# Row halves and column groups of TensorE for the small matmuls: softmax rounds over both KV groups, a reordered mLSTM output, and the router in four column groups

## The reference

```
proj = rms_norm(x) @ w_in            # attention q, k, v; mLSTM q, k, v, output gate; gates
att  = softmax(q k^T / 8 + bias, with a sink per head) v
                                     # 8 heads of 64, 2 KV groups of 4 heads, window of 128
h_m  = mLSTM(q_m, k_m, v_m, i, f)    # 4 heads, dqk 64, dv 128: per chunk
                                     #   num = scale * (q C) + (q k^T * decay) v, and its norm column
x    = x + concat(att, rms_norm(h_m) * sigmoid(o)) @ w_out
t    = rms_norm(x)
g_logits = t @ w_router_group        # 4 columns
e_logits = t @ w_router_expert       # 16 columns
x    = x + top-1 group, then top-2 of its 4 experts, SwiGLU experts of width 512
```

## Time and profile before

| | |
|---|---|
| median of 3 runs | 1065.3 us (1063.83 to 1066.48) |
| the profiled execution, its own time | 1064.2 us |
| its span in the profile | 1062.4 us |
| PE busy | 948.8 us, 89% |
| DVE busy | 618.2 us, 58% |
| ACT busy | 527.4 us, 50% |
| first stage (tiles) | up to about 433 us |
| second stage (output projection, router) | about 439 to 558 us |
| routing tables and first gather | about 553 to 590 us |
| experts | about 590 us to the end |
| granted TensorE clock, mean | 0.947 |

### The profile page before, as it was taken

One profiled execution on the slowest core, in us unless ns is written; L12 is line 12 of the kernel. 1 busy time (PEld: TensorE's weight loads), 2 busy tenths in 40 slices (PEclk: granted clock), 3 DMA queues, 4 the chain that ended last, 5 costly groups with the idle time before them and its releaser, 6 DMA issues. The chain is left out here.

```text
span 1062.4 us, 16918 instructions
## 1 busy us (share of the span) xinstructions
PE 948.8 (89%) x5026; PEld 792.8 (75%) x5027; DVE 618.2 (58%) x1245; ACT 527.4 (50%) x945; POOL 246.2 (23%) x362
## 2 busy tenths in 40 slices
PE   4789999999999969699971799999999999999993
PEld 3678889898888857588861577877877777787772
DVE  3646555656665565343367466447639489754891
ACT  3364644627455373122114356545638488664871
POOL 3101001010110100000017133243234345513452
PEclk9999999999999986899985799999999999999998
DMA  8620010101000050533463788678669799966963
GB/s 259 216 54 20 22 40 0 39 0 39 20 20 20 2 190 9 172 126 134 142 220 102 288 285 255 166 231 289 177 202 339 220 319 395 374 174 202 321 245 60
DMA packets 58122, 169.68 MB, mean 160 GB/s; under 512 B 12744, under 2 KB 15088, under 8 KB 58096
## 3 DMA queue, kind: packets, MB, share of 16 engines
q1 hardware_dynamic: 50384, 143.13, 37.5%
q0 software_dynamic: 7712, 26.24, 10.5%
HBM read 142.96 MB, written 26.38 MB: 159 GB/s over the span
## 5 line engine op out<-in xcount | busy, mean ns | idle before, releaser
L886 PE MATMUL bank_j<-w_high,rows_high 128*128 128x512 f32 x640 | 256.6, 401 | 11.7 <-DVE w_low L1327 9.4
L888 PE MATMUL bank_j<-w_high,rows_low 128*128 128x512 f32 x640 | 251.4, 393 | 0.0
L887 PE MATMUL bank_j<-w_low,rows_high 128*128 128x512 f32 x640 | 251.3, 393 | 0.0
L886 PEld LDWEIGHTS bank_j<-w_high,rows_high 128*128 128x128 f32 x640 | 121.2, 189 | 40.9 <-issue 12.3
L525 POOL TENSOR_TENSOR tick<-mhalf 1x1 f32<-1x1 f32 x146 | 83.9, 577 | 279.1 <-ACT lg L823 136.8
L888 PEld LDWEIGHTS bank_j<-w_high,rows_low 128*128 128x128 f32 x640 | 121.2, 189 | 26.1
L887 PEld LDWEIGHTS bank_j<-w_low,rows_high 128*128 128x128 f32 x640 | 121.6, 190 | 23.7
L1632 DVE TENSOR_TENSOR w_low<-w_res,w_high 128x1024 fp32r<-128x1024 f32 x96 | 112.8, 1219 | 13.8 <-ACT w_high L633 13.8
L633 ACT ACTIVATE w_high<-w_res 128x1024 fp32r<-128x1024 f32 x96 | 96.2, 1059 | 8.4 <-PE bank_j L888 8.0
L880 PE MATMUL bank_t<-ident,hn 128*128 128x128 f32 x328 | 45.1, 283 | 33.8 <-DMA hn<-ffn_in,row_g 22.2
L880 PEld LDWEIGHTS bank_t<-ident,hn 128*128 128x128 f32 x328 | 40.0, 146 | 39.0 <-issue 34.8
(11 more groups left out here) (301 smaller groups left out, 1823.0 us busy)
## 6 DMA issues: line engine op xcount, KB each, us to landing
w_res<-in_w_gate_dram SPq DMA_DIRECT2D x48, 512.0 KB, 4.9
w_res<-in_w_up_dram SPq DMA_DIRECT2D x48, 512.0 KB, 5.4
bias<-in_w_down_dram SPq DMA_DIRECT2D x32, 512.0 KB, 5.6
slot_b<-in_w_gate_dram SPq DMA_DIRECT2D x16, 512.0 KB, 5.7
PT<-in_w_up_dram SPq DMA_DIRECT2D x16, 512.0 KB, 5.9
gmix<-in_w_down_dram SPq DMA_DIRECT2D x16, 512.0 KB, 5.5
h<-in_w_down_dram SPq DMA_DIRECT2D x16, 512.0 KB, 7.2
hn<-in_x_dram SPq DMA_DIRECT2D x8, 512.0 KB, 3.5
```

The lines of the kernel that those rows point to most:

```text
L886: pe.matmul(out_, ah, bh, start=start, stop=False)
L887: pe.matmul(out_, ah, bl, start=False, stop=False)
L888: return pe.matmul(out_, al, bh, start=False, stop=stop)
```

## The change

Three edits, and what they need.

1. A softmax round r now holds two heads of each KV group: heads 2r and 2r+1 of group 0 (into S0) and of group 1 (into S1), and the matmuls alternate between the two row halves. `round_head` and `round_heads` give the head numbers and the strided slices of the per-head columns; `values`, `exps` and `logits` follow. The number and the sizes of the instructions on VectorE and ScalarE stay the same.
2. The mLSTM output first does the four products with 128 rows, then the four with 64 rows, which alternate between the row halves and the banks.
3. The router is turned round: its weights, padded from 20 to 32 columns, are stationary in one of four column groups (chunk k in group k % 4), the rows stream past, and the four partial sums land in four partition groups of X0[:, 0:128]. ScalarE copies them out (`router_parts`), and one more float32 matmul with a 0/1 matrix `rsel` adds them up (`router_sum`) into X0[:, 256:276]. For the tiles of the loop the router now stands before the second half of the output projection, its sum behind it. The padding of `wr` and the matrix `rsel` are made by GpSimd at the very start: two memsets and four affine selects more, and SyncE waits for them before it loads the router weights.

```diff
+        def round_head(r, j):
+            return (j // RH) * G + r * RH + j % RH          # RH = G // KVH = 2
+        def round_heads(per_head, r):
+            return per_head[:, :].rearrange("p (g r j) -> p g r j", g=KVH, r=G // RH)[:, :, r, :]
...
+            sp.wait_ge(pool_wr, 1)
...
+            chain(pool.memset(rsel[:, :], 0.0))
+            for q in range(4):
+                chain(pool.affine_select(out=rsel[:, :], in_=rsel[:, :], compare_op=ALU.not_equal, fill=1.0,
+                                         base=-q * WRC, pattern=[[-1, NG + NE]], channel_multiplier=1))
+            pool.memset(wr[:, :, NG + NE:], 0.0).then_inc(pool_wr, 1)
...
-                def scores(g, done):
-                    for j in range(G):
-                        b = (S0, S1)[j // 2]
+                def scores(r, done):
+                    for jj in range(RH):
                         for w, slot in ((0, v), (1, u)):
-                            c = (j % 2) * 2 * P + w * P
-                            ins = pe.matmul(b[:, c:c + P], qT[64 * g:64 * g + 64, j, :],
-                                            kTw[64 * g:64 * g + 64, slot, :], start=True, stop=True)
+                            c = jj * 2 * P + w * P
+                            for g, bank in enumerate((S0, S1)):
+                                ins = pe.matmul(bank[:, c:c + P], qT[64 * g:64 * g + 64, r * RH + jj, :],
+                                                kTw[64 * g:64 * g + 64, slot, :], start=True, stop=True)
...
                     for h in range(MH):
+                        c = h // 2
+                        pe.matmul((S0, S1)[h % 2][:, c * VE:(c + 1) * VE], sd[:, h, :], vm[:, h, :], start=(c == 0),
+                                  stop=False, skip_group_check=True)
+                    for h in range(MH):
                         r, c = 64 * (h % 2), h // 2
-                        o = (S0, S1)[h % 2][:, c * VE:(c + 1) * VE]
-                        pe.matmul(o, sd[:, h, :], vm[:, h, :], start=True, stop=False)
-                        ins = pe.matmul(o, qg[r:r + 64, c, :], Cst[r:r + 64, c, :], start=False, stop=True)
+                        ins = pe.matmul((S0, S1)[h % 2][:, c * VE:(c + 1) * VE], qg[r:r + 64, c, :], Cst[r:r + 64, c, :],
+                                        start=False, stop=True, skip_group_check=True)
...
                 for k in range(KC):
-                    ins = pe.matmul(X0[:, 0:NG + NE], h2T[:, k, :], wr[:, k, :], start=(k == 0), stop=(k == KC - 1))
-                ins.then_inc(pe_r, 1)
+                    q = k % 4
+                    ins = pe.matmul(X0[q * WRC:(q + 1) * WRC, 0:P], wr[:, k, :], h2T[:, k, :], start=(k < 4),
+                                    stop=(k >= KC - 4))
+                ins.then_inc(pe_rp, 1)
+
+            def router_sum(t):
+                pe.wait_ge(act_rp, t + 1)
+                pe.matmul(X0[:, 2 * P:2 * P + NG + NE], rpart[:, :], rsel[:, :], start=True,
+                          stop=True).then_inc(pe_r, 1)
...
                     mix_T(t + 1)
+                if not first and not last:
+                    router(t - 1)
                 if not first:
                     project_out(t, u, 1)
                 if last:
                     positions(TILES - 2, 1)
+                    router(t - 1)
                 if not first:
-                    router(t - 1)
+                    router_sum(t - 1)
...
+            def router_parts(t):                            # ScalarE, behind mix_high of body2
+                act.wait_ge(pe_rp, t + 1)
+                cp(rpart[:, :], X0[:, 0:P]).then_inc(act_rp, 1)
```

More of the change, by code:

```diff
@@ L116, in hymba_layer_program @@
         slot_b = sb("slot_b", [P, G * P + KVW + 64 + 2 * P + 2 * KVW])
-        wr = sb("wr", [P, KC, NG + NE])
+        WRC = P // 4
+        wr = sb("wr", [P, KC, WRC])
+        rpart = sb("rpart", [P, P])
+        rsel = sb("rsel", [P, NG + NE])
         ident = sb("ident", [P, P])
@@ L789, in body2 @@
                     mix_high(t + 1, 1 - u)
+                if not first:
+                    router_parts(t - 1)
                 act.wait_ge(dve_h, t + 1)
@@ L967, in probs_T, with values @@
                     ins.then_inc(done, 1)
-                def values(g, done):
+                def values(r, done):
                     for j in range(G):
-                        h = g * G + j
+                        h, g = round_head(r, j), j // RH
                         for w, slot in ((0, v), (1, u)):
@@ L1335, in out_low, with logits @@
                                          ALU.subtract).then_inc(lo0, 1)
-            def logits(t, g, s_done, l_done, nm_done):
-                hs = slice(g * G, g * G + G)
+            def logits(t, r, s_done, l_done, nm_done):
+                amx_r, anm_r, aes_r, sink_r = (round_heads(a, r) for a in (amx, anm, aes, sink))
                 dve.wait_ge(s_done, t + 1)
@@ L1348, in logits @@
                 dve.wait_ge(l_done, t + 1)
-                chain(dve.tensor_reduce(amx[:, hs], lg[:, :, :], AX, ALU.max))
-                chain(dve.tensor_tensor(amx[:, hs], amx[:, hs], sink[:, hs], ALU.max))
-                chain(dve.tensor_scalar(anm[:, hs], amx[:, hs], -1.0, None, ALU.mult))
-                dve.tensor_tensor(aes[:, hs], sink[:, hs], anm[:, hs], ALU.add).then_inc(nm_done, 1)
+                chain(dve.tensor_reduce(amx_r, lg[:, :, :].rearrange("p (g j) k -> p g j k", g=KVH), AX, ALU.max))
+                chain(dve.tensor_tensor(amx_r, amx_r, sink_r, ALU.max))
+                chain(dve.tensor_scalar(anm_r, amx_r, -1.0, None, ALU.mult))
+                dve.tensor_tensor(aes_r, sink_r, anm_r, ALU.add).then_inc(nm_done, 1)
             def body(t, u, main, nxt, ahead):
```

16 lines of the change are left out of this document (10 added, 6 removed).

## The result

The changed kernel takes 1034.6 us (median of 4 runs, 1031.3 to 1036.3), the kernel before beside it 1065.9 (4 runs, 1063.8 to 1067.9): ratio 0.9703, 95% interval 0.9672 to 0.9734. The prediction was 1033.0, with 1026 to 1042 as its range. The profiled execution took 1034.3 us, with a span of 1032.5.

What follows compares the result with a forecast made beforehand. TensorE, nearly always busy, was taken to bound the kernel. Savings of 22.3 + 3.3 + 5.0 + 1.7 = 32.3 us bring the profiled 1064.2 to 1031.9, forecast as a median of 1033.0 us, range 1026 to 1042.

Steps and rivals of the forecast that it cites:

- Score rounds: First-stage score rounds on TensorE: 1.98 to 1.09 us each, 0.2 us of waiting left, 1.58 us saved a tile.
- The bound of no overlap: Lower bound for the score rounds: saving 0 if the two row halves did not overlap.
- mLSTM output: First-stage mLSTM output group on TensorE: 3.29 to 1.67 us, saving 1.6 us, with VectorE still ready in time.
- Seven tiles: First-stage sum over seven tiles: 3.18 us saved in each, 22.3 us in all.
- Clock: First-stage tiles: one of three half-clock stretches fewer, 1.7 us saved; bounds 5.1 saved or several us lost.
- Last tile: Last first-stage tile: second score round saves 1.67 us, output 1.6, together 3.3; the DMA wait behind moves along.
- Second stage up to the tables: Second stage: five routers of 1.70 us become six of 0.68 and five sums, saving 3.3 us.
- The bound in which four column groups don't overlap: Second-stage router bound: all passes run singly, 2.2 us, a loss of 0.5 a tile.
- Tables: Routing tables: VectorE's wait of 1.39 us goes, plus some 0.3 of GpSimd's late wait of 0.66.
- Start: Program start: added GpSimd operations delay about 1.4 us, absorbed by TensorE's 1.49 us weight wait; cost 0, bounds 0 and 1.4.
- Other engines' chains: Rival, first stage: round 0's probabilities arrive too late, 0.7 us in seven tiles, 4.9 us back, 1038 us; chance 0.10.
- the rival: Clock falls oftener, in eight tiles and six router stretches: 11 falls more at 1.7 us, 1053 us; chance 0.08.

Runs made afterwards that it cites:

- e1: Kernel before with only the score rounds changed (both KV groups in alternating row halves): 1044.6 us, ratio 0.9825.
- e6: Changed kernel with each score round's matmuls not in turns, all of group 0 first, then group 1: 1039.4 us, ratio 0.9776 to the kernel before.
- e9: Kernel before with the new score rounds and the new mLSTM output order, without the router change: 1033.7 us, ratio 0.9733.
- e2: Kernel before with only the mLSTM output reordered (four products with 128 rows, then four with 64): 1060.0 us, ratio 0.9958.
- e10: The changed kernel measured again without any edit: 1028.9 us, ratio 0.9683 to the kernel before.
- e7: Changed kernel with all eight router matmuls in one column group and the sum over its 32 rows: 1044.5 us, ratio 0.9793 to the kernel before.
- e12: Changed kernel with ScalarE's copy of the router's partial sums moved behind the square, last body only: 1030.1 us, ratio 0.9671 to the kernel before.
- e4: Changed kernel with the six GpSimd operations moved from the start to behind the first tile's inverse root: 1028.7 us, ratio 0.9682 to the kernel before.
- e11: Changed kernel with the six GpSimd operations behind the first inverse root, measured again: 1028.4 us, ratio 0.968 to the kernel before.
- e5: Kernel before with only the six GpSimd operations at the start and the wait of the router's weight loads added: 1067.5 us, ratio 1.0007.
- e3: Kernel before with only the router changed, including its padding and `rsel`: 1063.5 us against 1066.3, ratio 0.9977.
- e8: Changed kernel with the router back behind the output projection's second half, its sum right behind it: 1032.9 us, ratio 0.9687 to the kernel before.

## Why the prediction was right, and where its steps were not

- **Score rounds: right.** 1.09 us and a wait of 0.18 for 1.09 and 0.2. e1 gives 1.64 us a tile, the step said 1.58. The bound of no overlap is excluded by e1, and e6 shows that the turns bring most of it. Line 1041 was the right row to go by. The Trainium skill, "TensorE: Matmul & The Clock Gate", Part 3, gives a measured 3.07 times for four packed row tiles. From that the prediction had estimated a round of 1.36 us; with two halves the trace shows no such loss, each pair takes one step of 0.11. (The price put on that estimate, some 4 us, was too high by its own rows: a round of 1.36 would have ended behind VectorE's copies, so the 0.2 of waiting would have gone, and 0.34 us a tile, some 3 us in all, would have been lost.)
- **mLSTM output: right**, 1.69 us for a forecast of 1.67, with VectorE still ahead. Shown by e9 less e1 (43.69 to 42.1). Its eight passes with 64 rows take 0.65 us (303.77 to 304.42), as line 1041 does, so the halves overlap here too. The surprise is e2: in its trace the same 1.6 us a tile is worth nothing (seven tiles take 322.2 us before and after), since the clock takes it.
- **Seven tiles: right**, 3.2 us each for 3.18 (26.9 us, less 4.6 for the falls, over seven).
- **Clock: the direction right, the size off.** The step took one fall fewer, 1.7 us. All three went, at 1.54 each: 4.6 us. The step had this among its bounds (5.1 if all three go). e1 shows that the score rounds do it. What rows show: no fall in the seven tiles of any kernel with rounds of 1.09 us (nine traces), two with 1.64 (e6), three or four with 1.98, and one in every tile with 1.98 and the shorter output. Why is not shown; that all three would go rather than one was not foreseen, and these 2.9 us are luck.
- **Last tile: 2.4 for 3.3 us, the size right and the wait behind it wrong.** The second round there, at half clock, takes 2.01 us (374.54 to 376.55) for a forecast of 2.04, and from the query transposes to the state update the tile is 3.3 us shorter (42.55 to 39.25). But the DMA wait behind it did not just move along, it grew by 0.84, as TensorE's rows before and after show:

```profile
439.32 1.94 PE L880 MATMUL bank_t<-ident,hn 128*128 128x128 f32 x8 [6.42 <-DMA hn<-mix_rows]
...
411.85 1.94 PE L907 MATMUL bank_t<-ident,hn 128*128 128x128 f32 x8 [7.26 <-DMA hn<-mix_rows]
```

  In e10 this wait is 6.30 us, and the stretch at half clock 17.1 us for 27.3; there the last tile gains 5.0. So what this tile is worth differs between executions.
- **Second stage up to the tables: right**, 3.5 us for 3.3, and 0.77 us a body for 0.80. The router was sized at 0.68 and the sum at 0.22, way in included; in the rows they take 0.58 and 0.14, and 0.20 more stand in the transposes ahead, 0.92 for 0.90 together. The bound in which four column groups don't overlap is excluded by e7 beside the change.
- **Tables: wrong.** The step had VectorE's wait of 1.39 us come out as time, 1.7 us with the late wait. The wait did vanish, but it was not on the path. First, VectorE's chain starts from the second half's end, which the router, now ahead of it, puts off: from the last transposes of mixed rows to `off_e` it takes 20.13 us (493.55 to 513.68) for 20.65 (524.55 to 545.20), only 0.5 less. Second, the first table write hangs on GpSimd's inverse root and so on ScalarE's square, and the new copy ahead of it holds that up. The prediction counted what the edit puts into TensorE's and GpSimd's queues, and passed over the copy in ScalarE's. e12 shows it: 0.8 us. The late wait of 0.66 falls to the 0.30 that stands before every write in e10 and e12, as forecast, but in the profile above the thirteenth write waits 1.41 us, where VectorE stood 1.16 us ahead of line 1347, and the copy of the rows on GpSimd took 7.01 us for 5.82. Neither is in e10, and their cause stays open. It is not the change's doing alone: four traces with the change's tables (e4, e6, e10, e11) take 64.4 to 64.5 us and never wait there, but e5, with the old router, waits 2.80 and takes 67.33, and e3 waits 2.28 and takes 67.07. Four traces with the old tables (before, e1, e2, e9) take 65.2 to 65.3. Undisturbed, the tables thus gain 0.7 us for the 1.7 forecast; the loss of 1.7 is of this execution.
- **Start: the mechanism right, the size off by little, and a fall unforeseen.** Cost 0 rested on TensorE's wait of 1.49 us for a weight DMA. It takes up most of the delay where no fall stands near 25 us (e8, e12: some 0.4 us is left, the operations taking 1.7 us and not the 1.4 of the upper bound; six operations 0.35 apart would have been 2.1). In the profile above line 1009 starts at 32.99 for 30.48, 2.5 us later, since the fall at 25.6 comes on top; whether the operations bring it on is open. e5's interval (-0.6 to +2.1 us) holds both 0 and 1.4.
- **Rivals.** Other engines' chains did not take over: TensorE waits 0.18 us in the tile's timeline. The clock did not fall oftener in the tiles, but e2 shows that the rival was real for an edit of this kind where the new score rounds are absent.

## What to carry to other kernels

In these traces plain float32 matmuls of 64 contraction rows run two for one when they take turns between the row halves and the banks (a round of 1.09 us for 1.98), and weights of 32 columns run four for one in four column groups (0.58 for 1.83, with 0.2 of way in on top of either). Look in the trace for a group that already has the pattern and size the new one by its step, start to start, and look at the neighbour ahead for the way in. Time an edit together with its neighbours too: one that saves 1.6 us a tile gave 4 us of 13 alone and its full price beside another. And for each copy that an edit adds, look at what stands behind it in that engine's queue at the end of the loop, where the order of the work is often another one.

## What the runs showed of the hardware

The half-clock stretches of the tiles hung on the small matmuls: with the output shortened and the score rounds old (e2), every tile had one of 3.4 or 6.8 us at a granted clock of 0.50, and a pair of tiles took 92.2 us as before; with score rounds of 1.09 us there were none in nine traces. With small matmuls unchanged and the first tile 3 us later (e5), the falls moved from the even tiles to the odd ones. Row halves overlap partly even when not issued in turns (e6: 1.64 us for 1.98). Two profiled executions of one kernel differ by 4 us through the length of one half-clock stretch (27.3 or 17.1 us) and some waits around the tables, which is five times what e12's edit is worth: edits of that size are read from the trace, not from the median.
